# PEER feed-forward of a hybrid decoder step: V of five token tiles as a dense product in a second phase

## The reference, cut to what matters

```python
D_MODEL, SEQ, DEC_BATCH = 1024, 1024, 8        # 1024 prompt tokens (8 tiles of 128) and 8 sample tokens
PEER_HEADS, N_KEYS, PEER_TOPK = 8, 128, 16     # 16384 experts, number = i1 * 128 + i2
...
def peer_ffn(h, w_q, sub_keys, u, v):
    ...
        eid = jnp.take_along_axis(cid, pos, axis=-1)            # (tokens, 8, 16) expert numbers
        gate = jax.nn.softmax(top_s, axis=-1)
        act = jax.nn.gelu(jnp.einsum('cd,chkd->chk', hc, u[eid]).astype(jnp.float32))
        return jnp.einsum('chk,chkd->cd', (gate * act).astype(v.dtype), v[eid])
```

## Time and profile before

| | us |
|---|---|
| median of 2 timed runs | 3359.82 (3357.81 to 3361.84) |
| profiled execution, its span from first to last instruction | 3436.9 |
| PE busy in it | 2499.1 |
| DVE busy | 2605.7 |
| ACT busy | 604.4 |
| POOL busy (issuing indirect DMAs) | 2333.0 |
| bytes moved | 1257.85 MB, mean 366 GB/s |

### The profile page before, as it was taken

How to read it: one execution, slowest core, us unless ns; L and a number is a source line. 1 busy time by engine, 2 the same in 40 slices (tenths; PEclk the granted TensorE clock), 3 DMA queues, 4 the chain that set the end, 5 groups by cost and what they waited for, 6 DMA issues and landing times.

```text
span 3436.9 us, 29857 instructions
## 1 busy us (share of the span) xinstructions
PE 2499.1 (73%) x7158; PEld 1274.5 (37%) x7158; DVE 2605.7 (76%) x6416; ACT 604.4 (18%) x1795; POOL 2333.0 (68%) x2076
## 2 busy tenths in 40 slices
PE   7957757888876788877766689977676545766665
PEld 4444335444433444433333344433332211333221
DVE  2268888788878888887867778887866688878754
ACT  1222221112222211211122111121121101111110
POOL 0047665677676777777777677777777676777775
PEclk9978868899866899998877899998887967898878
DMA  7969998999999999999999999999999999999997
GB/s 291 333 260 391 383 346 320 381 398 379 339 342 337 392 403 412 385 389 354 365 359 340 344 398 412 399 383 366 366 352 394 396 373 386 398 404 354 351 367 301
DMA packets 334308, 1257.85 MB, mean 366 GB/s; under 512 B 40736, under 2 KB 43640, under 8 KB 321696
## 3 DMA queue, kind: packets, MB, share of 16 engines
q0 software_dynamic: 298368, 1086.46, 82.8%
q1 hardware_dynamic: 35768, 169.50, 13.0%
HBM read 1247.04 MB, written 43.37 MB: 375 GB/s over the span
## 4 chain that ended last, share of the span: by engine, by line
POOL 30%; issue 17%; DVE 17%; PE 16%; DMA 12%; DVEq 5%; another core or an unknown queue 2%; ACT 1%; SPq 0%; ACTq 0%; POOLq 0%
POOL u_ring L1429 15%; POOL v_ring L1434 14%; DMA v_ring<-in_peer_v,idx 8%; PE acc L1703 7%; DVE u_ring L2316 5%; DVE accs L2354 4%; DMA u_ring<-in_peer_u,idx 3%; DVEq L2353 2%; PE pA L1633 2%; PE pS L1491 2%; PE pS L1610 1%; PE acc L1491 1%; PE pS L1543 1%; DMA wbuf<-in_w_out 1%
## 5 line engine op out<-in xcount | busy, mean ns | idle before, releaser
L1703 PE MATMUL acc<-v_ring,diag 128*128 128x512 f32 x2516 | 1384.2, 692 | 517.8 <-DMA v_ring<-in_peer_v,idx 340.6
L1429 POOL DMA_INDIRECT u_ring<-in_peer_u,idx x1024 | 1147.9, 1121 | 675.9 <-issue 305.2
L1434 POOL DMA_INDIRECT v_ring<-in_peer_v,idx x1024 | 1161.5, 1134 | 400.5 <-issue 287.3
L2316 DVE SCALAR_TENSOR_TENSOR u_ring<-u_ring,hb 128x1024 f32<-128x1024 f32 x1024 | 1235.0, 1220 | 228.9 <-DMA u_ring<-in_peer_u,idx 195.2
L1703 PEld LDWEIGHTS acc<-v_ring,diag 128*128 128x128 f32 x2516 | 514.3, 218 | 1225.5 <-issue 1091.4
L2354 DVE SCALAR_TENSOR_TENSOR accs<-v_ring,wv,accs 128x1024 f32<-128x1024 f32 x395 | 507.3, 1284 | 79.1 <-DMA v_ring<-in_peer_v,idx 29.9
L1944 ACT ACTIVATE diag<-idn,wv 128x128 f32<-128x128 f32 x629 | 233.5, 396 | 872.2 <-PE acc L1703 568.6
L1633 PE MATMUL pA<-T,wbuf 128*128 128x256 f32 (+2 forms) x1280 | 263.4, 363 | 22.2 <-issue 16.1
L1633 PEld LDWEIGHTS pA<-T,wbuf 128*128 128x128 f32 x1280 | 225.1, 208 | 75.6 <-issue 48.9
L1491 PE MATMUL pS<-wbuf,T 128*128 128x512 f32 (+1 forms) x424 | 176.2, 561 | 0.0
L1610 PE MATMUL pS<-wbuf,T 128*128 128x512 f32 (+1 forms) x288 | 136.6, 636 | 18.6 <-issue 13.0
(11 more groups left out here) (271 smaller groups left out, 2072.6 us busy)
## 6 DMA issues: line engine op xcount, KB each, us to landing
wbuf<-in_w_q SPq DMA_DIRECT2D x40, 1024.0 KB
out_dil_s<-in_cache_dil SPq DMA_DIRECT2D x8, 4092.0 KB
wbuf<-in_w_in SPq DMA_DIRECT2D x26, 1024.0 KB
wbuf<-in_w_out SPq DMA_DIRECT2D x20, 1024.0 KB
u_ring<-in_peer_u,idx POOLq DMA_INDIRECT x1024
v_ring<-in_peer_v,idx POOLq DMA_INDIRECT x1024
T<-in_xT_all SPq DMA_DIRECT2D x8, 512.0 KB, 13.5
accs<-in_x_all SPq DMA_DIRECT2D x8, 512.0 KB
```

The costliest lines, as they stand in the source:

```text
L1429: pool.indirect_dma_start(u_ring[:, entry % RU, :], None, table, bass.IndirectOffsetOnAxis(rows, 0))\
L1434: pool.indirect_dma_start(v_ring[:, entry % RV, :], None, peer_v, bass.IndirectOffsetOnAxis(rows, 0))\
L1703: m = pe.matmul(acc[0:R, half * 512:(half + 1) * 512], w, v_ring[:, entry % RV, half * 512:(half + 1) * 512], start=first, stop=last, skip ...
L2316: dve.scalar_tensor_tensor(row, row, 1.0, hb[:, t % ROWS, :], ALU.mult, ALU.mult, accum_out=dots[:, section % 2, j:j + 1]).then_inc(u_used, 1)
```

## The change

Tiles fall in three sets. FIRST = (0, 1) have V gathered as before, in the first phase. DENSE = ((2, 3, 4), (5, 6)) have V multiplied densely, group by group, in the second phase. LATE = (SAMPLE, 7) have V gathered in the second phase, from a ring of 4 (l_ring). The sample's u slots now come before tile 7's (AHEAD = 7 x 128).

**First phase.** All base work is due by place 400 (BASE_END). x2 of tiles 2 to 8 is stored to DRAM after "ox", h of tiles 2 to 7 after "oh", h comes back before the tile's dots (load_h). v_ring has 4 slots; the attention's scores and row maxima are double buffered for all tiles, and stages "v" to "vo", "q" to "qe", "k" to "ke" are kept together. At the end of the base work all engines drain and signal ("mark"), then the second phase's tiles take the SBUF of the base's tiles. POOL waits for the mark before the first late V gather.

**Second phase.** For a dense group of n tiles the experts are taken in 4 subs (halves of i1 by halves of i2: 64 x 64). A matrix M[expert block of 128, token] is made for the sub: 32 blocks x 128 tokens x n tiles, double buffered by sub. For 8 tokens at a time (a batch, 320 in all) DVE compares the picks' i1 and i2 with an iota (picks on partitions), ACT multiplies the first one-hot with the weight, PE multiplies the two one-hots (contraction over the 128 picks), ACT copies to M. Then PE multiplies M with peer_v, streamed from DRAM in chunks of 2 blocks x 512 columns (0.5 MB, two DMAs of SP, 4 buffers): 256 chunks in all, each group reads all of peer_v once. DVE adds the PSUM banks to accs after each half of D in each sub (16 times).

```diff
-RU, RV = 6, 7
+RU, RV = 6, 4
+FIRST = (0,1)
+DENSE = ((2,3,4),(5,6))
+LATE = (SAMPLE, 7)
...
+BUILDS = [(j, s, b) for j, group in enumerate(DENSE) for s in range(SUBS) for b in range(BATCHES * len(group))]
+SUMS = [(j, s, d) for j in range(len(DENSE)) for s in range(SUBS) for d in range(PASSES)]
+STREAM = [x + (c,) for x in SUMS for c in range(PAIRS)]
...
+                    out += [("dpc", t, 1.4) for t in group] + [("oc", n, 1.35) for n in batches]
...
+                    out += [("dpt", t, 0.5) for t in group] + [("om", n, 1.1) for n in batches]
...
+                        out += [("ow", n, 1.9)] + ([("oe", n - 1, 0.5)] if n > batches[0] else [])
...
+                    out += [("vd", m, 2 * len(group) * 0.48) for m in range(len(STREAM)) if STREAM[m][0] == j]
...
+            def load_h(t):
+                sp.wait_ge(hp_out, 16 * (t - KEPT + 1))
+                sp.wait_ge(u_used, DOTS_THROUGH[t - KEPT])
+                sp.dma_start(hb[:, t % KEPT, :], hp_scr[t * P:(t + 1) * P, :]).then_inc(hb_in[t % KEPT], 16)
...
+            def load_chunk(m):
+                j, s, d, c = STREAM[m]
+                need(sp, v_mm, m - NVS + 1)
+                for side in range(2):
+                    a = HALF * (s // 2) + QUARTER * side + 2 * c
+                    src = v_rows[a:a + 2, HALF * (s % 2):HALF * (s % 2) + HALF, 512 * d:512 * d + 512]
+                    sp.dma_start(vs[HALF * side:HALF * side + HALF, m % NVS, :, :],
+                                 src.rearrange("a b d -> b a d")).then_inc(vs_in[m % NVS], 16)
...
+            def fetch_v(p, rows):
+                late, entry = V_ENTRY[p]
+                ring_slot_free(V_FREE[late], entry, RL if late else RV)
+                if late and entry == 0:
+                    wait_base(pool)
...
+            def scatter(n):
+                pe.wait_ge(hot_w, n + 1)
+                need(pe, hot_e, n - 3)
+                out = staging(n)
+                for i in range(BATCH):
+                    for side in range(2):
+                        m = pe.matmul(out[HALF * side:HALF * side + HALF, QUARTER * i:QUARTER * (i + 1)],
+                                      hot2[:, n % 2, i, :], hotw[:, n % 2, i, QUARTER * side:QUARTER * (side + 1)],
+                                      start=True, stop=True, skip_group_check=True)
+                m.then_inc(hot_m, 1)
+
+            def dense_weigh(m):
+                j, s, d, c = STREAM[m]
+                if d == 0 and c == 0:
+                    pe.wait_ge(hot_e, BUILT[j, s])
+                if c == 0:
+                    need(pe, v_sum, m // PAIRS)
+                pe.wait_ge(vs_in[m % NVS], 32 * (m // NVS + 1))
+                for k in range(2):
+                    for u in range(len(DENSE[j])):
+                        x = pe.matmul(bank_of(u), M[:, (SUBS * j + s) % 2, u, 2 * c + k, :], vs[:, m % NVS, k, :],
+                                      start=(c == 0 and k == 0), stop=(c == PAIRS - 1 and k == 1))
+                x.then_inc(v_mm, 1)
...
+            def weight_columns(n):
+                j, s, b = BUILDS[n]
+                act.wait_ge(hot_c, n + 1)
+                need(act, hot_m, n - 1)
+                for i in range(BATCH):
+                    at = BATCH * b + i
+                    m = copy(hotw[:, n % 2, i, :], hot1[:, n % 2, i, :], turned[:, 2, at:at + 1])
+                m.then_inc(hot_w, 1)
...
+            def compare(n):
+                j, s, b = BUILDS[n]
+                dve.wait_ge(pair_e, PREPARED[DENSE[j][b // BATCHES]] + 1)
+                need(dve, hot_w, n - 1)
+                need(dve, hot_m, n - 1)
+                shape = [P, BATCH, HALF]
+                for half, of, out in ((s // 2, 0, hot1), (s % 2, 1, hot2)):
+                    m = dve.tensor_tensor(out[:, n % 2, :, :],
+                                          turned[:, of, BATCH * b:BATCH * (b + 1)].unsqueeze(2).broadcast_to(shape),
+                                          iota[:, HALF * half:HALF * (half + 1)].unsqueeze(1).broadcast_to(shape),
+                                          ALU.is_equal)
+                m.then_inc(hot_c, 1)
+
+            def dense_sums(i):
+                j, s, d = SUMS[i]
+                dve.wait_ge(dense_in, 16 * sum(len(group) for group in DENSE[:j + 1]))
+                dve.wait_ge(v_mm, PAIRS * (i + 1))
+                D_()
+                for u in range(len(DENSE[j])):
+                    row = accs[:, u, 512 * d:512 * (d + 1)]
+                    m = dve.tensor_tensor(row, row, bank_of(u), ALU.add)
+                m.then_inc(v_sum, 1)
```

712 lines of the change are left out of this document (528 added, 184 removed).

## The result

The changed kernel takes **4355.28 us** (median of 2 runs, 4349.94 to 4360.62) against 3359.82: ratio **1.297 [1.291, 1.304]**, 30% slower. The forecast was 3775, the range 3400 to 4060. The sign was right, the size short by 580 us, and most of it lies ahead of the first dense product: that came at 2456 us instead of 1949 (T1), 507 us late, and from there to the end 1892 us passed where 1870 had been worked out. 44 us more are what the forecast took off for a profiled execution that is longer than the timed ones: here the profiled span is 4348, no longer than the median.

A forecast was written before the change was run, and what follows sets the result against it. Before was taken as bound by gathered bytes, the changed kernel by PE after T1: 1949 us to T1 plus 1870 gave 3819, less 44, forecast 3775 us; own range 3640 to 3900, eight in ten 3400 to 4060.

The forecast's parts named there:

- T1: Moment when tile 4's weights exist and dense products can start; forecast 1949 us, from 3024 us of pooled PE and DVE work.
- 44 us: Taken off the end of 3819 us because the profiled execution of before ran 77 us longer than the timed ones.
- What bounds before, and the bytes: Whole kernel: before is bound by gathered bytes; net about 190 MB less, worth 0.47 ms of DMA time at 400 GB/s.
- 32 batches of tiles 2 and 3 that can be built early: Scatter work placed before T1: 32 batches at 1.38 + 1.9 us, 105 us of the pooled sum.
- the second rival: Scatter batches in rows cost PE ACT's 2.6 to 2.8 us instead of 1.9: 260 us more, 4035 us; chance 0.20.
- ACT's pace: Scatter: PE waits for eight scalings on ACT per batch, 2.6 to 2.8 us: 260 us more, 4035 us; chance 0.20.
- T1 to the end: PE after T1: scatter 547, dense 1101, late V 154, bank waits 48, tail 20; sum 1870 us.
- a batch is 1.9 us on PE: Scatter on PE: 32 passes at 0.054 us plus 0.16 for draining, per batch of 8 tokens.
- The others after T1: Second phase beside PE: DVE about 1020, ACT 780, DMA 1040 us; none reaches PE's 1870.
- Overlapping halves: Scatter: the two 64-column sides run together, a batch costs 0.95 us, 274 us less, 3500 us; chance 0.20.
- the favourable case: Whole kernel: scatter halves overlap and T1 comes at about 1800, giving 3356 us, no change; chance 0.07.
- PE not the bound: After T1: dense call 0.48 us and batch 1.1 as planned, end 3058 us, faster than before; chance 0.06.

The follow-up runs named there:

- e2: Changed kernel with dense products taking 256 of 512 columns; 4037.11 us, ratio 1.203 to the kernel before.
- e8: Changed kernel with dense groups (2), (3, 4), (5, 6), so peer_v is streamed three times; 4322.67 us, ratio 1.288 to the kernel before.
- e7: Changed kernel with half of PE's products left out in later groups' input, output and query projections; 4361.11 us, ratio 1.300 to the kernel before.
- e17: Changed kernel with DVE's dots and V sums at 64 columns, half of PE's base products, U/h gathers of 512 columns; 4188.45 us, ratio 1.220 to before.
- e1: Changed kernel with DVE's V sums of tiles 0 and 1 cut to 64 of 1024 columns; 4284.71 us, ratio 1.277 to the kernel before.
- e6: Changed kernel with dot products taking 512 of 1024 columns; 4189.43 us, ratio 1.249 to the kernel before.
- e9: Changed kernel with dots and DVE's V sums of tiles 0 and 1 cut to 64 columns; 4297.76 us, ratio 1.253 to the kernel before.
- e5: Changed kernel with dense groups (2, 3), (4, 5, 6); 4402.07 us, ratio 1.312 to the kernel before.
- e14: Changed kernel with ACT scaling 2 of 8 one-hots from the third batch on; 4347.36 us, ratio 1.257 to the kernel before.
- e18: Changed kernel with nothing edited, run again on the last chip; 4428.86 us, ratio 1.289 to the kernel before.
- e3: Changed kernel with every scatter product done twice; 4579.08 us, ratio 1.365 to the kernel before.
- e13: Changed kernel with dense products taking 32 of 512 columns; 4115.73 us, ratio 1.190 to the kernel before.
- e16: Changed kernel with dense products at 32 columns and the stream read in 4 KB instead of 2 KB pieces; 4148.25 us, ratio 1.199 to the kernel before.

## Why the prediction was wrong, step by step

**What bounds before, and the bytes.** Right as to bytes: 1071 MB, q0 751 MB. Wrong in what bytes cost: I took 400 GB/s for the stream. The packets of before took 0.828 x 3437 / 1086 = 2.6 us per MB on q0, and on q1, whose row is this,

```profile
q1 hardware_dynamic: 35768, 169.50, 13.0%
```

0.130 x 3437 / 169.5 = 2.6; now q0 takes 0.500 x 4348 / 751 = 2.9 and q1 0.236 x 4348 / 316 = 3.2, and the 147 MB that q1 gained take 579 us of all engines, 3.9 us per MB if the bytes it had before cost what they did. In sum the DMA engines' packets took 3293 us before and 3200 now: 187 MB fewer saved 93 us where 470 were reckoned. This did not set the time here, but it leaves a faster PE little to win (e2, e8).

**T1, the step that failed.** It was "Sum 958 + 677 + 824 + 39 + 421 + 105 = 3024 of two engines. At 85% of both ... T1 = 1949". Measured 2456, 507 us later. The terms first. From 170 to 2456 PE and DVE were busy 1420 and 1896 us, 3316 in all, 292 over the sum: base work on PE 1093 for 958 (the clock granted was 0.81, 0.69 and 0.50 in the three stretches, 0.84 from 170 us on in before; that fits, though no run separates it), DVE's base and sections 788 for 716, dots 846 for 824, V sums 431 for 421, 48 batches at 158 for 32 at 105. Three of these differences need a word. The prediction took the dots off DVE as 1235 + 84 us, but the two records of a dot overlap: the trace of before has 1242 us for both, so base work on DVE was 755 and not 677, and a dot costs 1.21 and not 1.29. With that put right DVE's base work came as in before. The 846 us hold 700 dots, 60 more than the forecast had up to T1. And the V sums split the other way round: 154 on DVE and 102 on PE, where 102 and 154 had been worked out. The largest real miss is PE's base work, 135 us.

By the prediction's own rate the 292 us are 292 / 1.70 = 172. The other 335 us are the rate: 3316 / 2286 is 1.45 engines, not 1.70.

The rate fell because the sum isn't one of interchangeable work. In before the plan could give each V sum to either engine at any time, and both together stood at 76 to 86% in the earlier trace rows. In the changed kernel this ends with tile 1 at 1376 us: the rest of the phase is dots for DVE and base for PE. The forecast took a rate from windows of a kernel with 1024 movable slots and put it on a phase with 256. I had written that PE would stand at 2 to 4 just before T1, and yet pooled the engines up to there. The fall from 81% to 64% when the V sums run out, and e7, where 171 us less on PE changed nothing, show that the pooling failed; which of the remaining limits sets the 1376 to 2191 stretch stays open (e17).

Nor would DVE's sum alone have served, though it comes near: its terms 677 + 824 + 39 + 131 + 44 = 1715 at the measured 83% give 170 + 2066 = 2236, still 220 early. And e1, e6 and e9 show that what is taken from DVE comes through by two fifths at most, in e9 by a sixth. What stands ahead of the first dense product is a row of stages: base work to 2191, the last dots and the weights of tile 4 to 2311, then 48 batches from 2317 to 2456, 2.9 us each. By the forecast's own words for T1, "when tile 4's weights exist", it came at 2311, 362 us late, and the batches after it are the rest. This last part holds two more errors of the step. "32 batches of tiles 2 and 3 that can be built early" can't be before the mark (e5, e8), and the written list holds them for tile 4 after it. And with no dense products between them they stand in rows, as the second rival had it, though not at ACT's pace (e14). DVE and ACT are busy 131 and 113 of 143 us there, and neither sets the time by itself (e9, e14):

```profile
2313.00:2456.00 143.00, 95.10 (x1572) 88.24 (x1572) 130.79 (x232) 112.90 (x447) 68.39 (x59) 0.50 0.70 220
```

The forecast had counted 32 batches as 105 / 1.70 = 62 us of pooled work, and 16 more after T1 at 1.9; 48 took 139.

**T1 to the end.** Right in sum: 1892 (1946 in e18) for 1870, PE bound, 90% busy. Its terms: dense products 1119 for 1101, 0.437 us a pass as the earlier trace rows had it, and not the plan's 0.48 a call; late V 212 for 154, as PE took 95 slots and not 82, at 2.2 us; the scatter 393 for 547. The last is an error of its own: I took 0.054 us a pass by the length of 64-column loads, and a pass costs 0.037 (e3), between that and the 0.030 of overlapping halves. What it gave was taken back by waits: PE idled 182 us for the 68 of stalls and tail, 123 of them for the scalings. So the term "a batch is 1.9 us on PE" came out as (393 + 123) / 272 = 1.9 for the wrong reason, and 272 batches were left where I had 288. The Trainium skill (TensorEngine Tiling (Array Packing), Key Properties) says that tiles load and multiply independently and that a change of mode drains the array. The pass of 0.037 fits a part of the first; no run here separates the drain.

**The others after T1.** DVE 842 for 1020 (332 dots and 272 batches were left where I had 392 and 288), ACT 659 for 780 (a scaling lasts 0.335 us, but they overlap, and 2560 of them keep ACT busy for 645: 0.25 each for the 0.28 interpolated), DMA at 0.69 and 204 GB/s. None bounds it, as foretold.

**The rivals.** Overlapping halves came in part (0.037 us a pass for the 0.030 priced) and were eaten by the waits; the favourable case fell with T1. ACT's pace holds in part: the batches ahead of the first dense product take 2.9 us each, though only 12 of their 139 us go with ACT's scalings (e14), and PE waits 123 us after it, where 260 had been priced. PE not the bound fell: e2 shows dense time to be PE time. The case that came, a first phase that the sum does not describe, stood in no rival; the range was that of T1 "by 100 us". The remark at the end, wrong "if T1 lies outside 1850 to 2150", named the right sign. The 44 us for the profiled execution are a term without a ground: the kernel before alone takes 3353 to 3465 us in the five groups, so 77 us between two of its executions lie within what the groups differ by.

## What to carry to other kernels

A pooled sum over two engines is only allowed while the stretch holds work that either may take; ask for each stage how much of it is left and when it runs out, and beyond that sum each engine by itself and look for the chain of stages. Where a written list puts a whole group's preparation ahead of its first piece of work, the last member of the group sets the start of all. Where a change sets a barrier between two phases, the parts of the sum that lie on either side of it add up, and what is to be built "early" must be free of the barrier's memory. And bytes saved are to be weighed by the engine time of the queue that they come back on.

## What was not expected of the hardware

- In e13 PE's dense products are cut to 32 columns, PE is still busy for 1248 of 1639 us, and the granted clock is 0.60, most of it at the lower level (1.2 GHz), where e2 has 0.84 with 1252 of 1575. From the base end to the first dense product the clock is 0.50 throughout, with PE busy 97 of 265 us; through the 48 batches in rows, 94 of 139 us busy, it stayed there, and in e3, with PE busy for 174 of 176 us with such passes, it was 0.50 too. The Trainium skill (TensorE: Matmul & The Clock Gate, Part 1) ties the clock to how busy the PE has been; by the profile's busy time these runs don't fit that simply, since e13 and e2 differ little in it (76 and 80% of the stretch) and e3's row is busy throughout at the lower level.
- The passes of the scatter (64 columns of weights, 32 streamed) cost 0.037 us each at the margin at a granted clock of 0.88 (e3). At clock 0.50, 64 of them a batch took 176 us for 48 batches in e3, 0.057 us a pass.
- The DMA engines were full at 251 and 283 GB/s in e8 where stream and gathers ran side by side, against 362 to 406 in before; pieces of 4 KB for 2 changed nothing that can be told from the noise (e16).
